# V's weights loaded in four quarters of rows, with the first six products of V taken together by those quarters

## The reference, cut to what matters

```python
mod = silu_c @ w_ada[l] + b_ada[l]                      # (B, 6D)
sh_m, sc_m, gt_m, sh_f, sc_f, gt_f = jnp.split(mod[:, None, :], N_MOD, axis=-1)
h = rmsnorm(x, g_pre_mix[l]) * (1 + sc_m) + sh_m
p, q1, q2, k1, k2, v = project(h, w_in_l)               # w_in: 2048 x 4096, [pool | q | k | v]
attn = diff_attend_blocked(q1, q2, k1_all, k2_all, v_all, lam)
mix = jnp.concatenate([pool, attn...], axis=-1) @ w_out[l]
x_new = x + gt_m * rmsnorm(mix, g_post_mix[l])
x_new = x_new + gt_f * rmsnorm(swiglu(h2, w_gate_up[l], w_down[l]), g_post_ffn[l])
```

## Time and profile before

| | us |
|---|---|
| median of 3 runs | 1865.48 (1863.57 to 1865.65) |
| the profiled execution | 1873.23 |
| its span on the slowest core, core 4 | 1871.7 |
| spans of the eight cores | 1841.2 to 1871.7 |
| PE busy on core 4 | 1755.3 (94%) |

### The profile page before, as it was taken

The page is one execution under the profiler, slowest core; times in us unless marked ns, Lnnn a source line. Parts: engine busy times, 40 slices in busy tenths (PEclk is TensorE's granted clock), DMA queues, the critical chain, the costliest instruction groups (busy, mean ns, idle before and its releaser), DMA issues.

```text
span 1871.7 us, 28333 instructions; the slowest of 8 cores (1841.2 to 1871.7 us)
## 1 busy us (share of the span) xinstructions
PE 1755.3 (94%) x11435; PEld 906.1 (48%) x11574; DVE 578.0 (31%) x1317; ACT 518.1 (28%) x826; POOL 111.0 (6%) x119
## 2 busy tenths in 40 slices
PE   1369999999999999999999999999999999999997
PEld 1225545544656777654444444444444444444443
DVE  2123357667734444455531110111001110101033
ACT  2033310000279899974540000000000000101011
POOL 1000000000000011000010000000000000000000
PEclk9578889999999999999999999999999999999999
DMA  9976774024648888794396664664665743454547
GB/s 197 161 188 157 151 142 69 1 37 62 95 70 152 153 149 149 127 163 151 135 160 88 90 82 55 88 86 61 79 90 66 101 85 62 70 86 65 90 129 240
DMA packets 155472, 205.11 MB, mean 110 GB/s; under 512 B 3120, under 2 KB 133584, under 8 KB 148432
## 3 DMA queue, kind: packets, MB, share of 16 engines
q0 software_dynamic: 146224, 145.24, 52.3%
q1 hardware_dynamic: 9120, 58.06, 9.1%
HBM read 331.72 MB, written 16.79 MB: 186 GB/s over the span
## 4 chain that ended last, share of the span: by engine, by line
PE 85%; DMA 7%; ACT 3%; another core or an unknown queue 3%; issue 2%; DVE 1%; DVEq 0%; SPq 0%; ACTq 0%; POOLq 0%
PE ps L311 84%; DMA arena<-w_ada 3%; ACT arena L284 2%; DMA out<-arena 2%; PE ps L315 1%; DMA arena<-xa 1%; DMA arena<-w_in 1%; DMA arena<-xscr 1%; DVE arena L299 0%; ACT sml L284 0%; DVE arena L290 0%; SPq L318 0%; ACT L284 0%; DVEq L1003 0%
## 5 line engine op out<-in xcount | busy, mean ns | idle before, releaser
L311 PE MATMUL ps<-arena 128*128 128x512 bf16 (+4 forms) x9397 | 1702.3, 342 | 36.3 <-ACT arena L284 14.8
L311 PEld LDWEIGHTS ps<-arena 128*128 128x128 bf16 x9536 | 818.9, 99 | 868.0 <-issue 178.4
L284 ACT ACTIVATE arena<-ps 128x1024 bf16<-128x1024 f32 (+5 forms) x500 | 396.3, 836 | 1077.6 <-PE ps L311 1073.1
L290 DVE TENSOR_TENSOR arena<-arena,ps 128x512 bf16<-128x512 f32 (+1 forms) x92 | 61.6, 670 | 537.1 <-PE ps L311 535.1
L290 DVE TENSOR_TENSOR arena<-ps,arena 128x512 f32<-128x512 f32 x80 | 54.4, 680 | 212.1 <-ACT arena L284 212.0
L290 DVE TENSOR_TENSOR arena<-arena 128x512 f32<-128x512 f32 (+7 forms) x128 | 109.7, 857 | 9.2 <-DVE arena L299 1.4
L299 DVE SCALAR_TENSOR_TENSOR arena<-arena,sml 128x128 f32<-128x128 f32 (+2 forms) x224 | 84.8, 405 | 67.9 <-ACT sml L284 38.3
L284 ACT ACTIVATE arena<-arena 128x2048 bf16<-128x2048 f32 x27 | 51.5, 1908 | 146.6 <-DMA arena<-xa 103.4
L315 PE MATMUL ps<-identsb,arena 128*128 128x128 bf16 (+1 forms) x502 | 44.5, 240 | 48.4 <-DVE arena L294 22.5
L318 POOL DMA_DIRECT2D arena<-w_gu x44 | 50.3, 1145 | 631.8 <-PE ps L311 515.1
L311 PE MATMUL ps<-cpair,arena 128*128 128x1 bf16 (+1 forms) x1536 | 67.8, 164 | 20.5 <-DMA arena<-w_ada 20.1
(11 more groups left out here) (42 smaller groups left out, 192.4 us busy)
## 6 DMA issues: line engine op xcount, KB each, us to landing
arena<-w_gu POOLq DMA_DIRECT2D x44, 1024.0 KB, 10.7
arena<-w_ada POOLq DMA_DIRECT2D x32, 1024.0 KB, 10.5
arena<-xa SPq DMA_DIRECT2D x27, 1024.0 KB, 8.3
arena<-w_dn POOLq DMA_DIRECT2D x16, 1408.0 KB, 10.6
arena<-w_ada POOLq DMA_DIRECT2D x8, 2048.0 KB, 23.9
arena<-w_in POOLq DMA_DIRECT2D x6, 2048.0 KB, 18.8
arena<-w_out POOLq DMA_DIRECT2D x4, 2048.0 KB, 23.9
xscr<-arena SPq DMA_DIRECT2D x8, 1024.0 KB, 5.0
```

The source lines that it names most:

```text
L284: P.op("act", lambda e: e.activation(out, in_, func, **kw), rd, wr)
L290: P.op("dve", lambda e: e.tensor_tensor(out, a, b, op), [a, b], [out])
L311: P.op("pe", lambda e: e.matmul(out, lhsT, rhs, start=start, stop=stop, skip_group_check=skip), [lhsT, rhs], [out], signal=signal)
```

## The change

The two halves of V's weights now lie in one buffer `V_AB` of 16 row blocks by 1024 columns, loaded by four DMAs, each of four row blocks and all 1024 columns: 4 KB contiguous in HBM in place of 2 KB. None of them waits for another. `K_1` takes row blocks 0 to 7 of that buffer, so its load is issued behind the loop in place of behind step 33.

The first six products (tiles 2, 3, 4 with both column halves) are taken together: for each quarter of the rows, four matmuls for each product, into six banks. Their ACT moves stand in steps 0 to 5. The chains of tiles 6 to 9 move from steps 0, 1, 4, 5 to 6, 7, 8, 9 and load into four new buffers `xst2` (in the place of `scb[0]` and `scb[1]`); tiles 10 and 11, in steps 11 and 12, find the two old ones free. The late loads wait for the last quarter of `V_AB`. The rounds of pair (6,7) all stand behind step 7, those of pair (8,9) behind 9, 10, 11 and 11. The first load of `shb` moves from step 1 to step 9 and hangs on tile 9's buffer; its `col_mm` moves from step 12 to 13. The chains of tiles 12 to 17 are now spread over steps 14 to 21.

```diff
-        V_A, V_B, K_C = slot16(A_), slot16(B_), slot16(KT0 + 18432)
+        V_AB = region(A_, 16384, BF16).rearrange("p (k n) -> p k n", k=16)
+        V_A, V_B = V_AB[:, :, 0:512], V_AB[:, :, 512:1024]
+        K_C = slot16(KT0 + 18432)
+        xst2 = [region(HO + i * 8192, 2048, F32) for i in range(4)]
...
-        for hf in (0, 8):
-            dma("pool", V_A[:, hf:hf + 8, :], w_in_v[:, hf:hf + 8, 3072:3584])
-        for hf in (0, 8):
-            dma("pool", V_B[:, hf:hf + 8, :], w_in_v[:, hf:hf + 8, 3584:4096], after=[V_A[:, hf:hf + 8, :]])
+        for q in range(4):
+            dma("pool", V_AB[:, 4 * q:4 * q + 4, :], w_in_v[:, 4 * q:4 * q + 4, 3072:4096])
...
-            xs = xst[n % 2] if i != 18 else xst[1]
+            xs = xst2[i - 6] if 6 <= i < 10 else xst[i % 2] if i != 18 else xst[1]
...
-            dma("sp", xs, xa[i * 128:(i + 1) * 128, :], after=[V_B[:, 0:8, :]] if late else ())
+            dma("sp", xs, xa[i * 128:(i + 1) * 128, :], after=[V_AB[:, 12:16, :]] if late else ())
...
-        seq = [(i, 0) for i in (2, 3, 4, 5)] + [(i, 1) for i in (2, 3, 4, 5)]
+        seq = [(i, c2) for i in (2, 3, 4, 5) for c2 in (0, 1)]
+
+        vfirst = (0, 1, 2, 3, 6, 4)
+        for q in range(4):
+            for (i, c2), b in zip(seq, vfirst):
+                src, lo = hTs(i)
+                for kc in range(4 * q, 4 * q + 4):
+                    mm(bank(b), src[:, kc, lo:lo + 128], V_AB[:, kc, c2 * 512:(c2 + 1) * 512], kc == 0, kc == 15,
+                       signal=(kc % 4 == 3))
...
-        for p, s0 in ((2, 4), (3, 8), (4, 12), (5, 16), (6, 20)):
+        for r in range(4):
+            rounds.setdefault(7, []).append((2, r))
+        for r in range(4):
+            rounds.setdefault((9, 10, 11, 11)[r], []).append((3, r))
+        for p, s0 in ((4, 12), (5, 16), (6, 20)):
...
-        chains = {0: 6, 1: 7, 4: 8, 5: 9, 8: 10, 10: 11, 12: 12, 14: 13, 16: 14, 17: 15, 18: 16, 19: 17, 24: 0, 25: 1, 32: 18}
-        shq = {12: 0, 18: 1, 23: 2, 28: 3}
+        chains = {6: 6, 7: 7, 8: 8, 9: 9, 11: 10, 12: 11, 14: 12, 15: 13, 17: 14, 18: 15, 20: 16, 21: 17, 24: 0, 25: 1, 32: 18}
+        shq = {13: 0, 18: 1, 23: 2, 28: 3}
...
-            if s == 1:
-                dma("pool", shb, w_ada_v[:, 0:4, 0:2048], after=[xst[1]])
-            v_step(i, c2, V_A if c2 == 0 else V_B)
+            if s == 9:
+                dma("pool", shb, w_ada_v[:, 0:4, 0:2048], after=[xst2[3]])
+            if s < 6:
+                v_evac(i, c2, vfirst[s])
+            else:
+                v_step(i, c2, V_A if c2 == 0 else V_B)
...
-                dma("pool", V_A, w_in_v[:, :, 2560:3072])
...
+        dma("pool", K_1, w_in_v[:, :, 2560:3072])
         dma("pool", Q_0, w_in_v[:, :, 1024:1536])
```

More of the change, by code:

```diff
@@ L429, in proj, with v_evac @@
             return b
+        def v_evac(i, c2, b):
+            act(V[:, i, 4 * c2:4 * c2 + 4, 0:128], bank(b).rearrange("p (h e) -> p h e", h=4), AF.Identity)
         def v_step(i, c2, wslot):
-            b = proj(i, wslot)
-            act(V[:, i, 4 * c2:4 * c2 + 4, 0:128], bank(b).rearrange("p (h e) -> p h e", h=4), AF.Identity)
-        seq = [(i, 0) for i in (2, 3, 4, 5)] + [(i, 1) for i in (2, 3, 4, 5)]
+            v_evac(i, c2, proj(i, wslot))
+        seq = [(i, c2) for i in (2, 3, 4, 5) for c2 in (0, 1)]
[6 more added lines that the diff above has]
+                       signal=(kc % 4 == 3))
         for p in range(2, 6):
@@ L533, in halo @@
                        modc[:, 16 + kc:17 + kc], ALU.mult, ALU.add)
-        K_0, K_1, Q_0, Q_1 = K_C, V_A, V_B, V_A
+        K_0, K_1, Q_0, Q_1 = K_C, slot16(A_), slot16(B_), slot16(A_)
+        dma("pool", K_1, w_in_v[:, :, 2560:3072])
         dma("pool", Q_0, w_in_v[:, :, 1024:1536])
```

## The result

The changed kernel takes 1844.44 us (median of four runs, 1838.64 to 1847.0) where the kernel before takes 1865.19: 20.8 us less, ratio 0.9886 with a 95% interval of 0.9862 to 0.991. The forecast was 1842.5. The profiled execution took 1838.6 us, its span on core 0 is 1837.1, the eight cores lie between 1824.5 and 1837.1. In the mean over the cores the span fell from 1855.5 to 1833.1, by 22.4. In the profile of the kernel before, cores 4 and 5 were granted 0.81 for most of the time from 111 to 272 us, and in this one no core was; over the other six cores the mean fell from 1852.0 to 1832.5, by 19.5.

The account below looks back on a forecast made before the run. PE bounds the kernel (85% of the chain), so only the beginning can shorten: product 13's end moves from 165.8 to 142.6, later terms about even. 1865.5 - 23.0 = 1842.5 us, range 1833.5 to 1852.5.

Parts of the forecast that it names:

- The sum: Whole kernel: 23.2 us gained by product 13's end on core 4, 23.0 in all, time 1842.5; chance 0.64.
- The three waits: PE before product 13's end: 3.33 us for V_A's second half, 7.95 for a bank move, 8.75 for tile 9.
- The third wait: PE's 8.75 us at the first round of pair (8,9), wanting tile 9, whose load waits for shb's 2 MB.
- Quarters of V: V's load: 26 us, 6.5 a quarter, landing by 77.3, 83.8, 90.3 and 96.8; run length worth 0 to 1.8.
- Where PE starts: Start of PE on V: at 77.3 us as before, since as many bytes are due.
- Six products by quarters: First 96 matmuls on PE: done at 102.0 us, with 0.8 waited for the last quarter; bounds 101 and 118.3.
- Tiles: Late loads: tiles 6 to 9 there at 102, 105, 108, 111; shb asked for at 111, there by 131.
- rival (b): Six tile loads share the rings and all land at about 117; gain 12 us, time 1853; chance 0.10.
- Pair (6,7) and steps 8 to 13: PE waits 0.4 us, starts product 8 at 114.3, waits 0.4 for tile 9, ends product 13 at 142.6.
- Behind step 13: Waits for the shift's loads: nothing to 1 us on core 4; 6.8 us on core 0, 8.1 before.
- rival (c): Shift's loads need 27 us against 19.5 of five steps; full-clock cores wait 16.5; gain 15, time 1850; chance 0.11.
- rival (e): Clock: an earlier dense start puts cores at 0.81 sooner and longer; 250 us of it ends at 1900; chance 0.03.

Follow-up runs that it names:

- e2: Changed kernel with its first six products one after another in place of together by quarters; 1859.8 us, ratio to before 0.9924.
- e3: Changed kernel with tiles 6 to 9 in the two old buffers and the first shift load tied to the second; 1855.19 us, ratio to before 0.9898.
- e5: Kernel before with only V's weights changed to one buffer in four 4 KB-run quarters, K_1's load behind the loop; 1860.6 us, ratio 0.9965.
- e6: Kernel before with the first shift load hanging on tile 7's normalized copy, so tile 9 no longer waits for it; 1864.24 us, ratio 0.9974.
- e1: Changed kernel with each quarter of V loaded by two DMAs of 2 KB runs, and more semaphores; 1847.5 us, ratio to before 0.9862.
- e9: Changed kernel with lambda's step, including two small row loads, in step 10 in place of 6; 1842.32 us, ratio to before 0.9883.
- e10: Kernel before with the two small row loads issued early, right behind tile 5's, nothing else moved; ratio to before 0.9994.
- e8: Changed kernel with the first shift col_mm in step 12, tile 9's chain in step 8 and tile 11's in step 11; 1844.17 us, ratio to before 0.9879.

## Why the prediction was right, point by point

- **The sum.** Forecast -23.0, measured -20.8; the ratio's interval is 17 to 26 us. At the end of product 13, where 23.2 was forecast, the gain is 24.2 on core 4 (165.8 to 141.6) and 20.9 in the mean over the six cores that were not at 0.81 before (159.7 to 138.8); 1.0 of the 2.3 that are missing there is the later start of V. That core 4 came out so near is partly luck: it began 2.9 us late and had full clock instead of 0.81, which by the prediction's own two numbers (142.6 and 139) gives 3.6 back.
- **The three waits as the source.** All three are gone. The experiments show two of the replacements by themselves: without the products by quarters PE waits 13.0 us and 16.8 us of time come back (e2); with two tied buffers 8 to 13 us of wait and 12.2 us of time (e3). The second wait, a product's move standing behind tile 6's Square, has no experiment of its own: that moving the chains behind the moves took it away is read from ACT's rows. Adding the three waits, as my first paragraph did, was only a way to see where to look: e5 and e6 show that one taken away changes the others. The third wait was misread in part: it was the last round of pair (6,7) waiting for a bank behind tile 9's work in DVE's queue, as the rows with e6 show, and not the first of pair (8,9) waiting for the tile. The cause that the change removes, tile 9's load tied to `shb`, is the same.
- **Quarters of V.** I took 26 us for the load, 0 to 1.8 of it for the run length. From the last `col_mm` at 73.92 to the tile loads at 98.82 it took 24.9: for the run length the experiments give 0.9 us (e5, three quarters in 19.2 us against 19.9, scaled to four) to 2.5 (e1) where I had 0 to 1.8. In time e1 cost 4.5 us, which is more than this term. The Trainium skill (DMA: Bandwidth & Descriptors, Specifications) puts line rate from 512 B on, by which it would have given 0; here the measurement decides.
- **Where PE starts.** This step failed: "PE starts at 77.3 as before: as many bytes are due". It started at 80.22 on core 4, 1.2 to 2.1 us later in the mean. I had counted V's bytes and not the two small loads that the change moves ahead of the tiles into the load of w_ada, though the order of SP's queue shows them. e9 and e10 show this as the cause. What it costs in time is less than the shift of the start: e9 did not end clearly sooner.
- **Six products by quarters.** Start to end of product 7 was forecast as 33.1 us (77.3 to 110.4, with 0.81 on the last two) and took 31.4 (80.22 to 111.67). At full clock the forecast would have been 31.6. The waits in it were 2.2 us for V, forecast 0.8. The first 96 matmuls were done by 105.0, when ACT began the sixth move, 3 us after the forecast 102.0, as the start was.
- **Tiles.** Forecast at 102 to 111, 3 us apart; on core 4 they landed at 105.1, 108.5, 112.0 and 115.4, in turn and not together, against rival (b). The shift's load, which waits for tile 9, left 17.2 us after the first tile's issue on core 4 (98.82 to 115.97) and 13.4 on core 1, where 14 were forecast. ACT waited for none of the four on core 4, and at most 0.69 us for any of them on the others. I count that as no cost.
- **Pair (6,7) and steps 8 to 13.** Wait 1.29 instead of 0.4 before the rounds, then 3.6 us to product 8's start (113.18 to 116.81) as forecast 3.5; 1.29 and 0.40 for tiles 9 and 11, for 0.4 and 0. These are the smaller steps at full clock, which shorten PE's cover. Product 13 ended at 141.56 for 142.6 (at 0.81) or 139 (full clock).
- **Behind step 13.** Core 0 waited 4.89 + 0 + 1.50 = 6.4 us, forecast 6.8. Core 4 was forecast to wait at most 1 us and waited 6.7, at full clock and not at the 0.81 of the forecast. In the mean the waits for `shb` rose from 1.3 to about 5 us: rival (c) is at work, with a third of the 16.5 us of waits that it was priced with.
- **The clock.** No core was at 0.81 in any profile of the changed kernel, against rival (e) and against the rule of the Trainium skill that I had cited with it (TensorE: Matmul & The Clock Gate, Part 1: The HAM clock gate): PE was busy for 397.4 us or more of the 400 from 800 to 1200 on all eight cores, and the granted clock was 1.00. PE was nearly full on all eight cores there, as it was in the profile of before on the two cores at 0.81. Why cores 4 and 5 were at 0.81 early in that profile stays open. The runs add that a pair of cores with a lower mean clock is found in six of 27 runs of the kernel before and seven of ten of e6, and in none of the changed kernel; such runs took some 7 to 13 us longer. The forecast took core 4's 0.81 as lasting, and corrected for it only at the end, by the median.

## What to carry to other kernels

When loads and products start together, take several products through each piece of the weights as it lands, and let nothing that waits for a later load stand ahead of the moves that free the banks, on ACT or on DVE. Look at every buffer that a load is tied to: a tie to save a semaphore or order a queue can cost half of what the whole change gains (e3, e6). Before a point that a load fixes, waits do not add up, so name the next late thing before counting a wait as gain; and cost the small DMAs that an edit moves, not only its large ones.

## What the runs showed of the hardware that I had not expected

- Two loads that spread one row over 128 partitions, 128 and 64 KB as written, take 15.7 to 22.5 us to land among large loads (nine profiles), and with them early the last scale `col_mm` begins 1.6 us later in the mean over the cores (71.7 against 70.1, nine and five profiles). In the window 20:40 of the slowest core SP's queue had 34.9 to 45.7% of the engines with them and 30.2 to 33.2% without.
- With them early, the two cores of a pair drift up to 6.3 us apart in the load of w_ada (68.0 and 74.3 in e8).
- V's casting loads moved 4.19 MB in 24.9 us with 4 KB runs (24.7 to 26.0 in the nine profiles with the tile loads behind the whole of V) and in 27.4 with 2 KB runs (e1).
- Two neighbouring cores can be held at 0.81 while the six others are not (cores 4 and 5 in the profile of before, 111 to 130 and 141 to 272 us). This was seen in one of fourteen profiles.
